# A two-layer stream encoder on one core: a depthwise convolution's request taps of two channel tiles as products on ScalarE and sums on GpSimd, and VectorE's work behind them in another order

## What is computed

```python
proj = h @ w_in
a_val, a_gate, z, xbc, dt_raw = jnp.split(proj, [...], axis=-1)
a_glu = a_val * jax.nn.sigmoid(a_gate)
a_conv, new_conf_state = causal_dwconv(a_glu, conf_state, conf_w, conf_b)   # 31 taps, 512 channels
a_out = jax.nn.silu(layernorm(a_conv, ln_g, ln_b))
xbc_c, new_xbc_state = causal_dwconv(xbc, ssd_conv_state, xbc_w, xbc_b)     # 4 taps, 1024 channels
xbc_c = jax.nn.silu(xbc_c)
```

## Time and profile before

| | |
|---|---|
| median of 3 runs | 1724.46 us (1724.01 to 1724.63) |
| the profiled execution's own time | 1724.16 us |
| its span, first to last instruction | 1722.2 us |
| TensorE busy | 1676.7 us, 97% |
| VectorE busy | 1059.8 us, 62% |
| ScalarE busy | 719.1 us, 42% |
| GpSimd busy | 418.8 us, 24% |
| mean granted TensorE clock | 0.997 |
| TensorE's share of the chain that ended last | 81% |

### The profile page before, as it was taken

One profiled execution on the slowest core, in us unless ns is written; L12 is line 12 of the kernel. 1 busy time (PEld: TensorE's weight loads), 2 busy tenths in 40 slices (PEclk: granted clock), 3 DMA queues, 4 the chain that ended last, 5 costly groups with the idle time before them and its releaser, 6 DMA issues.

```text
span 1722.2 us, 28511 instructions
## 1 busy us (share of the span) xinstructions
PE 1676.7 (97%) x11696; PEld 1590.0 (92%) x11696; DVE 1059.8 (62%) x1709; ACT 719.1 (42%) x1289; POOL 418.8 (24%) x327
## 2 busy tenths in 40 slices
PE   7999888999999999999999999999999999999999
PEld 6989876897999999999989898789799999999999
DVE  3899957547677646465654335654666774655564
ACT  4322564244434435253542135533543452534352
POOL 3424421221004233232223033100110241414240
PEclk9999999999999999999999999999999999999999
DMA  8323440242213131303133223503330313122312
GB/s 265 105 90 90 124 160 7 74 194 101 86 39 129 47 130 32 129 26 129 37 130 74 75 74 110 203 27 145 125 105 19 123 48 133 44 73 84 101 53 92
DMA packets 40253, 164.96 MB, mean 96 GB/s; under 512 B 9448, under 2 KB 10344, under 8 KB 26176
## 3 DMA queue, kind: packets, MB, share of 16 engines
q1 hardware_dynamic: 32816, 127.21, 22.4%
q0 software_dynamic: 7312, 35.98, 5.8%
HBM read 152.49 MB, written 10.42 MB: 95 GB/s over the span
## 4 chain that ended last, share of the span: by engine, by line
PE 81%; DVE 4%; ACT 1%; issue 1%; POOL 0%; DVEq 0%; ACTq 0%
PE G L991 57%; PE S L991 12%; PE Q L991 11%; PE Q L1717 1%; ACT work L1813 0%; DVE ev_low L2732 0%; DVE stats L2762 0%; DVE resid L3014 0%; ACT h_split L1813 0%; PE Q L1429 0%; DVE stats L3133 0%; DVE work L2775 0%; ACT front L1813 0%; DVE w_split L2987 0%; ACT rstd L1813 0%
## 5 line engine op out<-in xcount | busy, mean ns | idle before, releaser
L991 PE MATMUL G<-ffn_rows,w_split 128*128 128x320 f32 x2160 | 329.8, 309 | 0.0
L991 PEld LDWEIGHTS G<-ffn_rows,w_split 128*128 128x128 f32 x2160 | 320.1, 188 | 0.0
L1813 ACT ACTIVATE w_split<-ring 128x512 fp32r<-128x512 f32 (+2 forms) x224 | 159.1, 711 | 316.5 <-PE G L991 208.1
L907 POOL TENSOR_TENSOR mkT<-ring 128x512 f32<-128x512 f32 x72 | 98.5, 1373 | 564.2 <-DMA ring<-in_w_up 384.3
L991 PE MATMUL G<-h_split,w_split 128*128 128x320 f32 x1344 | 200.9, 310 | 1.2 <-DVE w_split L2492 0.9
L991 PEld LDWEIGHTS G<-h_split,w_split 128*128 128x128 f32 x1344 | 197.5, 188 | 1.9 <-issue 1.3
L991 PE MATMUL G<-g_split,w_split 128*128 128x320 f32 x1056 | 163.7, 310 | 0.1
L991 PEld LDWEIGHTS G<-g_split,w_split 128*128 128x128 f32 x1056 | 156.6, 188 | 1.6 <-DVE w_split L2987 1.3
L2854 DVE TENSOR_TENSOR w_split<-ring,w_split 128x512 fp32r<-128x512 f32 (+1 forms) x124 | 104.7, 846 | 61.2 <-ACT w_split L1813 60.0
L2987 DVE TENSOR_TENSOR w_split<-ring,w_split 128x512 fp32r<-128x512 f32 (+1 forms) x80 | 65.5, 818 | 115.6 <-ACT w_split L1813 114.8
L2576 DVE SCALAR_TENSOR_TENSOR S<-front,par,S 128x512 f32<-128x512 f32 x232 | 107.0, 546 | 0.1
(11 more groups left out here) (365 smaller groups left out, 3277.0 us busy)
## 6 DMA issues: line engine op xcount, KB each, us to landing
ring<-in_w_up SPq DMA_DIRECT2D x44, 1024.0 KB, 4.8
ring<-in_w_down SPq DMA_DIRECT2D x48, 256.0 KB, 2.7
ring<-in_w_down SPq DMA_DIRECT2D x32, 320.0 KB, 2.9
front<-in_mem_k POOLq DMA_DIRECT2D x8, 1024.0 KB, 7.1
front<-in_mem_v POOLq DMA_DIRECT2D x8, 1024.0 KB, 11.1
resid<-in_x SPq DMA_DIRECT2D x8, 640.0 KB, 9.2
ring<-in_w_mk SPq DMA_DIRECT2D x4, 1024.0 KB, 5.8
ring<-in_w_mv SPq DMA_DIRECT2D x4, 1024.0 KB, 11.0
```

The source lines that it names most:

```text
L907: nc.gpsimd.tensor_tensor(wsum[n], a, b, ALU.subtract).then_inc(sum_ready, 1)
L991: return nc.tensor.matmul(out, lhsT, rhs, start=start, stop=stop, **kw)
L1813: return nc.scalar.activation(*a, **k)
```

## The change

For gate tiles 2 and 3 the 128 request columns leave VectorE. ScalarE multiplies each of the 31 shifted rows by its tap (the first with the bias added) into a buffer of four products, which is a batch (`step_products(j, batch)`, eight batches a tile, the last of three). GpSimd adds the batches into the first one (`step_taps(j, batch)`, L848 of the changed kernel), and after the eighth adds the four partial sums in two steps (L852, L854) and raises `step_sum`. Two product buffers alternate, so ScalarE waits for GpSimd's sum of the batch two before (`step_tap`). Tile 3 starts in the same buffer as tile 2, so its first batches wait for `step_sum`. VectorE keeps the request taps of gate tiles 0 and 1 and all prompt taps, and takes the prompt taps of tiles 2 and 3 in turn; `step_sizes` stands behind the tenth tap of these. The mean's sums move behind xbc tile 0, `decay_sums` from ahead of xbc tile 4 to ahead of tile 2, the sum of the squares from ahead of tile 4 to ahead of tile 5. On ScalarE `xbc_first(0)` and all `xbc_silu` move forward, the squares stay ahead of `xbc_rows(7)`, and on TensorE the mean's `conv_stat` stands after tile 12.

```diff
+            def step_taps(j, batch):
+                done = 8 * (j - 2) + batch
+                count = min(4, CW - 4 * batch)
+                pool.wait_ge(step_rows, 8 * (j - 2) + batch + 1)
+                if batch > 1:
+                    pool.wait_ge(step_tap, done - 1)
+                total = tap_sum[:, 0:count, :]
+                nc.gpsimd.tensor_tensor(total, total, tap_rows[batch % 2][:, 0:count, :], ALU.add).then_inc(step_tap, 1)
+                if 4 * batch + count == CW:
...
+                    nc.gpsimd.tensor_tensor(acc[:, j, SEQ:T], tap_sum[:, 0, :], tap_sum[:, 1, :], ALU.add)\
+                        .then_inc(step_sum, 1)
+            step_taps(2, 1)
             memory_keys(1)
-            for n in range(8, 10):
-                front_low(n)
+            for batch in range(2, 5):
+                step_taps(2, batch)
+            front_low(8)
+            for batch in range(5, 8):
+                step_taps(2, batch)
+            front_low(9)
+            step_taps(3, 1)
             for j in range(KD):
                 front_low(10 + j)
+                if j < 3:
+                    step_taps(3, 2 * j + 2)
+                    step_taps(3, 2 * j + 3)
...
-                if n == 14:
+                if n == 12:
                     conv_stat(3)
...
+            def step_products(j, batch):
+                out = tap_rows[batch % 2] if batch else tap_sum
+                if batch > 2:
+                    act.wait_ge(step_tap, 8 * (j - 2) + batch - 2)
+                elif batch == 0:
+                    read_wait(act, TILE0["glu"] + 2 * j + 1)
+                if batch < 3 and j > 2:
+                    act.wait_ge(step_sum, j - 2)
+                for w in range(4 * batch, min(4 * batch + 4, CW)):
...
+                        ins = A(rows, src, ACT.Copy, scale=pr("cw", j * CW + w))
+                ins.then_inc(step_rows, 1)
...
             memory_values(1, 1)
+            for j, batch in ((2, 5), (2, 6), (2, 7), (3, 0), (3, 1)):
+                step_products(j, batch)
...
             xbc_rows(2)
             front_high_part(12)
+            step_products(3, 6)
+            step_products(3, 7)
+            xbc_first(0)
+            xbc_first(1)
             xbc_rows(3)
...
+            both_taps(1, 14, CW)
+            for w in range(CW):
+                if w == 10:
+                    step_sizes()
+                for j in (2, 3):
+                    conv_tap(j, w, 0)
...
             for j in range(KD):
+                if j == 1:
+                    dve.wait_ge(conv, 6 * CW)
+                    conv_sum(0, lambda k: k < 2 or dve.wait_ge(step_sum, k - 1), lambda k: acc[:, k, :])
+                if j == 2:
+                    decay_sums()
                 if j == 3:
                     subtract_mean()
-                if j == 4:
-                    decay_sums()
+                if j == 5:
                     conv_sum(3, lambda k: dve.wait_ge(sq_ready, 24 + k + 1), lambda k: sq[:, k % 2, :])
```

More of the change, by code:

```diff
@@ L376, in build @@
         xdt, xdte, btok = [r(512)], [r(512)], [r(256)]
+        tap_sum, *tap_rows = (v.rearrange("p (w t) -> p w t", w=4) for v in (hT, xdt[0], xdte[0]))
         dt_rows = r(4, T)
@@ L1963, in front_high_part @@
                 ins.then_inc(front_high, 1)
+            def step_products(j, batch):
[7 more added lines that the diff above has]
+                for w in range(4 * batch, min(4 * batch + 4, CW)):
+                    rows, src = runs(out[:, w % 4, :]), padded(aglu, j, 0, CPROMPT, CREQ, w)[1]
+                    if w == 0:
+                        ins = A(rows, src, ACT.Identity, scale=pr("cw", j * CW), bias=pr("cb", j))
+                    else:
+                        ins = A(rows, src, ACT.Copy, scale=pr("cw", j * CW + w))
+                ins.then_inc(step_rows, 1)
             memory_values(0, 0)
@@ L1984, in _ @@
             evacuate(dt_parts, TILE0["dtp"])
+            for batch in range(2):
+                step_products(2, batch)
             log_exp_table()
             head_norms(lambda j: mkT[:, 1, j, :], TILE0["mk1"], 4, 1.0 / P, MT)
+            for batch in range(2, 5):
+                step_products(2, batch)
             front_high_part(8)
@@ L2055, in _ @@
                 square(acc[:, k, :])
+            xbc_silu(3)
             xbc_rows(7)
             front_high_part(17)
-            xbc_silu(3)
+            xbc_silu(4)
             z_gate(0)
             front_high_part(18)
-            xbc_silu(4)
+            xbc_silu(5)
             log_exp_table()
@@ L2067, in _ @@
             front_high_part(19)
-            xbc_silu(5)
+            xbc_silu(6)
+            xbc_silu(7)
             log_exp_table()
@@ L2075, in _ @@
                 .then_inc(read[n % 2], 1)
-            for j in range(6, KD):
-                xbc_silu(j)
             z_gate(2)
@@ L2559, in subtract_mean, with conv_tap, both_taps, gate_rows @@
                 nnorm[0] += 1
-            taps_done = [0]
-            def conv_taps(count):
-                for at in range(taps_done[0], taps_done[0] + count):
-                    j, w, i = at // (2 * CW), at % (2 * CW) // 2, at % 2
-                    part = (S[:, 0, :], runs(S[:, 1, 0:NS]))[i]
-                    out = (acc[:, j, 0:SEQ], runs(acc[:, j, SEQ:T]))[i] if w == CW - 1 else part
-                    src = padded(aglu, j, 0, CPROMPT, CREQ, w)[i]
-                    tap = pr("cw", j * CW + w)
-                    if at >= 2:
-                        dve.wait_ge(conv, at - 1)
-                    if w == 0:
-                        ins = v.tensor_scalar(out, src, tap, pr("cb", j), ALU.mult, ALU.add)
-                    else:
-                        ins = v.scalar_tensor_tensor(out=out, in0=src, scalar=tap, in1=part,
-                                                     op0=ALU.mult, op1=ALU.add)
-                    ins.then_inc(conv, 1)
-                taps_done[0] += count
-            dve.wait_ge(pads_in, 16 * 12)
-            dve.wait_ge(small_ready, 3)
-            for j in range(4):
+            tap_at = {}
+            def conv_tap(j, w, i):
+                part = (S[:, j % 2, :] if j >= 2 else S[:, 0, :], runs(S[:, 1, 0:NS]))[i]
+                out = (acc[:, j, 0:SEQ], runs(acc[:, j, SEQ:T]))[i] if w == CW - 1 else part
+                src = padded(aglu, j, 0, CPROMPT, CREQ, w)[i]
+                tap = pr("cw", j * CW + w)
+                if w == 0:
+                    if j:
+                        dve.wait_ge(conv, max(at for (old, _, _), at in tap_at.items() if old < max(j, 2)))
+                    ins = v.tensor_scalar(out, src, tap, pr("cb", j), ALU.mult, ALU.add)
+                else:
+                    dve.wait_ge(conv, tap_at[j, w - 1, i])
+                    ins = v.scalar_tensor_tensor(out=out, in0=src, scalar=tap, in1=part,
+                                                 op0=ALU.mult, op1=ALU.add)
+                ins.then_inc(conv, 1)
+                tap_at[j, w, i] = len(tap_at) + 1
+            def both_taps(j, first, end):
+                for w in range(first, end):
+                    for i in range(2):
+                        conv_tap(j, w, i)
+            def gate_rows(j):
                 n = TILE0["glu"] + 2 * j
@@ L2591, in _ @@
                 read_wait(dve, n + 1)
-                conv_taps(32 if j < 3 else 44)
-            step_sizes()
-            conv_taps(8 * CW - taps_done[0])
+            dve.wait_ge(pads_in, 16 * 12)
+            dve.wait_ge(small_ready, 3)
+            gate_rows(0)
+            both_taps(0, 0, 16)
+            gate_rows(1)
+            both_taps(0, 16, CW)
+            both_taps(1, 0, 1)
+            gate_rows(2)
+            both_taps(1, 1, 14)
+            gate_rows(3)
+            both_taps(1, 14, CW)
[4 more added lines that the diff above has]
+                    conv_tap(j, w, 0)
             def conv_sum(first, ready, part):
```

25 lines of the change are left out of this document (16 added, 9 removed).

## The result

The change made the kernel slower: 1727.62 us against 1724.17 in the same series (medians of 16 runs each), a ratio of 1.0022 with an interval of 1.0015 to 1.0029. The forecast was 1719.6, so the sign was wrong. The runs of the changed kernel also lie further apart, 1724.90 to 1729.99 against 1722.54 to 1724.79. The profiled execution took 1728.07, with a span of 1726.3 (1722.2 before).

A forecast was written before the change was run, and what follows sets the result against it. TensorE, busy 97% of the span, was taken as the bound, so only its waits and slow stretches could be won. 12.4 - 2.1 - 2.7 - 3.0 = 4.6 us gained, 1724.16 - 4.6 = 1719.6 us; range 1715.0 to 1724.0.

The forecast's parts named there:

- The old wait: TensorE's waits for GpSimd's low parts at tiles 17 and 16, 10.3 us; with 2.1 of slow clock, 12.4 us removed.
- B: Ahead of tile 9, TensorE waits for its low part, which stands behind five additions on GpSimd: 2.7 us lost.
- No wait came at tiles 10 to 13: The other batches of products and additions stay covered by TensorE's tiles: nothing lost, though the cover is thin.
- C: Ahead of tile 17, TensorE waits because VectorE's sum of squares ends late: 3.0 us lost, none without contention.
- A: TensorE's second value tile waits for the buffer that VectorE's later step sizes free: 2.1 us lost.
- the clock falls in the new gaps: Rival: each of three new TensorE gaps costs 2.1 us of clock, 1721.7 to 1725.9; 22%, shared with C and A high.
- 1.1 for each low part: Contention price for VectorE's chain beside GpSimd's low parts 13 to 16; with half that for tile 3's last additions, 5.0 us.
- No row prices that: Said for the rival that decay sums hardly mind low parts, so C is nothing: 1716.6 us, 22%.
- the slower rival: Five meetings each hold VectorE a whole 2.5 us low part; C is 10.5, clock 2.1 more: 1729.2 us, 6%.
- if nothing holds tile 17 or tile 16: Condition under which the whole 12.4 us at these TensorE tiles was counted as removed.
- Behind tile 17: nothing: After tile 17, ScalarE's and VectorE's work up to the scan moves with TensorE: nothing more gained or lost.

The follow-up runs named there:

- the run in eighths: Changed kernel with step sizes behind four prompt taps instead of ten, and GpSimd's low parts 13 to 16 each as eight 128x128 subtractions instead of two 128x512: 1716.34 us.
- both runs with zeros: Changed kernel with GpSimd writing zeros for low parts 13 to 16: 1719.53 us; the same with step sizes behind four prompt taps instead of ten: 1713.05 us.

## Why the prediction was wrong

**Right.** The old wait went, and B's wait was 2.70: products at 2.48 for eight, additions at 3.88 for three, 0.74 and 0.46, as worked out. The step sizes' readout came at 138.03 where 137.6 was worked out. No wait came at tiles 10 to 13. C had VectorE's sum of squares at its root. With A and the contention taken away the time was 0.2 us from the sum of the remaining terms and the 1.55 us below.

**A, mis-sized: 2.1 forecast; taking it away gave 5.9, of which 1.55 are a gain that the sum lacked, so 4.3 in the sum's terms.** The position of the step sizes was right. The value tiles reached the place 1.55 us earlier than in the trace of before, so TensorE waited 3.73. That alone would have cost what was forecast, 3.73 - 1.55 = 2.2. The rest is the clock: the value tile behind the gap took 10.19 us in this profile and 8.65 to 8.86 in three others, where 7.17 is a tile at a clock of 1.00.

The forecast overlooked where the 1.55 come from. VectorE's last gate rows stood behind 48 pairs of taps and now stand behind 45. Before, the first key tile of TensorE, which takes the buffer that they read, starts at 111.61, just behind them:

```profile
110.63 0.68 DVE L2588 TENSOR_TENSOR front<-work,G 128x512 f32<-128x512 f32 x1
111.61 7.15 PE L991 MATMUL G<-front,ring 128*128 128x256 f32 x32 [1.36 <-issue]
```

After, VectorE is there 2.6 us earlier, and TensorE's 1.36 us of idle time are gone:

```profile
107.99 0.68 DVE L2650 TENSOR_TENSOR front<-work,G 128x512 f32<-128x512 f32 x1
110.03 7.17 PE L1020 MATMUL G<-front,ring 128*128 128x256 f32 x32
```

The list of waits doesn't have that idle time, because the profile names no releaser for it. No run tests it by itself.

**The step that failed first is the rival "the clock falls in the new gaps"**, which was set aside with "9.1 us is the only long gap of this stretch, and these are a third of it". A missing row was taken as evidence. In the profile all three gaps lowered the clock, 3.0 + 1.4 + 1.5 = 5.9 us together, the largest part of the 8.5 us that the time lay above the forecast. With three losses that rival gave 1725.9, and 2.5 us for tile 16 and for the longer wait at tile 17 make it 1728.4, where the profiled execution took 1728.07. There the Trainium skill (TensorE: Matmul & The Clock Gate, Part 1) was read as allowing one such loss; the trace shows three, with full tiles between them.

**The second failed step is the price "1.1 for each low part", a mean over 24 taps.** The chain lost 8.2 us, not 5.0. That mean came from a stretch of xbc taps, in which the 512-column ones, most of VectorE's time there, are not held: 0.74 to 0.76 us beside a low part as without. In the new order one of the mean's sums, a cast, and a copy and a product on eight partitions lie there, and none of them was done before a subtraction ended: low parts 13 to 16 cost 3.1, 1.8, 2.0 and 0.9. "No row prices that" had been said of the decay sums, and the low value was taken all the same. The rule of the Trainium skill (SBUF — State Buffer, "Who interferes with whom") agrees with the rows better than the mean does: the cast that ends with the low part, and eighths that hold VectorE briefly. It would have spoken for a C between the forecast and the slower rival.

**Forgotten: tile 16.** The sum took the whole 10.3 us away ("if nothing holds tile 17 or tile 16"), with 1.2 of it at tile 16. Its high part stands behind `xbc_silu(2)`, which needs VectorE's late chain, so 1.3 us remained there. With the contention away it went, too.

"Behind tile 17: nothing" was right to 1.2 us.

## What to carry to other kernels

Price a new gap ahead of TensorE with the time at a lower clock behind it, above all where a trace has one long gap whose cost is known: here gaps of 2.7 us cost nothing or about 1.4 us more than their wait, and gaps of 3.7 to 4.2 us some 1.5 to 3.0 more. When an engine's work moves beside GpSimd's two-input instructions, price each meeting by what is left of GpSimd's instruction, and cut that into short pieces before moving more work, as in the run in eighths. A wait at the end of a chain moves on when only the queue that shows it is reordered; ask first what makes the chain late.

## What the runs showed of the hardware

The same gap does not always lower the clock. Eight profiles have the wait of 2.67 to 2.70 us at tile 9. In five of them the lowest window of five microseconds behind it has a clock of 0.67 to 0.78 (the changed kernel, squares late, low parts on VectorE, eighths, step sizes at tap 9), and in three it is 1.00 (step sizes early, and both runs with zeros). Behind A's 3.7 us the clock fell every time, and the tile took 10.19, 8.65, 8.86 and 8.76 us in four profiles. That would account for the wider spread of the changed kernel's runs; it was not tested by itself.

VectorE instructions with a single tensor operand in SBUF were held, too: a cast of 128x8, 0.16 us alone, took 1.25, and a copy of 8x4 took 1.17. The cast, the copy and the product of 8x96 ended within about 0.1 us of the end of a subtraction of GpSimd. The sum that took 3.90 us had begun 0.67 us ahead of the low part of tile 13 and was held through both of its subtractions all the same. Beside GpSimd's writing of zeros two of the mean's sums took 1.76 us and twelve scans 2.04; beside the eighths the same twelve scans took 3.74.
